# A recurrent block computed as three rounded products in place of one full one, with both halves of its input projection ahead of the gates

## The chip, the cores and the metric

The kernel runs on one core of one Trainium2 chip. The metric is the device time in microseconds (us), lower is better. One launch computes everything.

## The reference, cut to what matters

Two pairs of blocks follow each other over 512 tokens of width 1024, in float32. The first block is a recurrent mixer; a token's `h` is its normed input with a scale and a shift that depend on a condition vector `c` (the modulation).

```
mod = cond @ ada_w[i] + ada_b[i]             # six vectors of 1024: shift, scale, gate, twice
h = rmsnorm(x, norm_mix_g[i]) * (1.0 + sc1) + sh1
u = h @ w_in                                 # 1024 -> 2560
xb, gb = jnp.split(u, 2, axis=-1)
gate = jax.nn.gelu(gb)
xc = conv(xb, 4 taps) + conv_b
r = sigmoid(xc @ wr + br);  i = sigmoid(xc @ wi + bi)      # five blocks of 256 x 256
a = exp(-8 * r * softplus(-lam))
b = sqrt(1 - a*a) * (i * xc)
hs[t] = a[t] * hs[t-1] + b[t]
x = x + g1 * ((hs * gate) @ w_out)           # 1280 -> 1024
```

A feed-forward block, a sparse attention block and another feed-forward block follow; then an "even" block (768 tokens, latent and context: input projection of 21 tiles, a convolution of five taps, silu, and a norm of each head), its attention parts, an odd block and two more feed-forward blocks.

## The kernel before

Features lie on the 128 partitions and tokens along the row, so a tensor of 1280 features is ten tiles of 128 x 512. Each stage is a function that returns five programs, one for each engine's queue (`sp`, `pe`, `act`, `dve`, `pool`); a queue runs in the order in which it is written, and all order between engines is by semaphores (`st.at(event)`). So the order of the calls is the schedule. The weights stream through two slots of 2 MB (`panels`), 32 tiles of 128 x 128 each, in the order of `weight_plan`; a slot is loaded again when its last reader is done.

There are two kinds of matrix product. `linear` multiplies float32 by float32: one MATMUL in the code, two records in the profile. `linear3`, `turn3` and `opening3` multiply numbers split in a rounded high part and a rest (type fp32r): high by high, high by rest, rest by high, three MATMULs, one record each. For these the weights are made ready in groups of eight tiles: ACT rounds a group (`Halves.act`, one instruction of 128 x 1024) and POOL subtracts to get the rest in the weight slot itself (`HalvesInPlace.pool`, one instruction of 128 x 1024). Before the change every big projection but the recurrent block's `a_in` (20 output tiles by 8) and `a_out` (8 by 10) is of the second kind.

The recurrent block (`rglru`) before, on PE: eight products for the norm's sum; `a_in` tiles 0 to 3 in two halves of the inner index (L821), tiles 4 to 9 (L563); the gates, 20 outputs of two products each (L833); `a_in` tiles 10 to 19 (L563), the gelu branch; `a_out` (L563). DVE has the modulation (`Modulation.dve`, L396: two long multiply-and-sum instructions for each of 24 halves), the scaling of h, the taps of the convolution (L943, L946), and after the gates `gated_x` (L950), `m_product` (L955), the recurrence (L958 and the scan L960), and the end of gelu and its product with the scan (L963, L965). ACT has the gates' tanh (L884), two more functions of each (L889, L891), the roots (L894) and gelu's tanh (L900). POOL squares `a` (L982) and makes gelu's argument (L987, L989, L991). The scans, and gelu's work, run while PE is at tiles 10 to 19. 

In the even block a tile passes through ACT (copy, first tap), DVE (four taps, L2064), ACT (tanh), DVE (silu, L2070), and then the norm of its heads, `hn`: a square on ACT (L1414), a sum on PE (L1423), logarithm and exponential on ACT (L1432, L1435, with an exchange of the function table ahead of and behind them, L1995 and L2011), a product on DVE (L1442). `hn` for tile `i` stands on ACT in the round of tile `i + 2`, on PE ahead of the products of tile `i + 3` and on DVE in the round of tile `i + 3`. ACT copies tile `mt + 1` out of its bank only when it has squared tile `mt`.

Of the kernel before, what the change touches and what calls it, by code (L numbers as in the profile page):

```python
# [7 lines left out]
F32 = mybir.dt.float32  # L8
# [20 lines left out]
def weight_plan():  # L29
# [21 lines left out]
    stat("a_in", 10, 8)  # L51
# [4 lines left out]
    stat("a_in", 10, 8, 10)  # L56
    stat("a_out", 8, 10)
# [257 lines left out]
SPLIT = ("b_in", "b_out", "f1_0", "f2_0", "f1_1", "f2_1", "g_0", "u_0", "d_0", "g_1", "u_1", "d_1", "e_in", "e_out", "o_in", "nav", "gv", "o_out")  # L315
# [30 lines left out]
class Modulation:  # L346
# [19 lines left out]
    def landed(self, t):  # L366
        return (self.early[t][1], 16) if t < len(self.early) else (self.sems[t % 2], 16 * (self.base + t // 2 + 1))

    def sp(self, e, at):

        t = at["t"]
        if t < 2 * len(self.jobs):
            if t >= len(self.early) + 2:
                e.wait_ge(*self.st.at("half", t - 2))
            q = self.jobs[t // 2][0]
            e.load(self.slot(t), self.d_ada[q, :, (t % 2) * 2048:(t % 2 + 1) * 2048]).then_inc(self.landed(t)[0], 16)
            at["t"] += 1

    def dve(self, v, at, D):
# [4 lines left out]
        j, half = divmod(t, 2)  # L384
# [19 lines left out]
def program(nc, d_w, d_ada, d_const, d_rope, d_par, d_cond, d_rpb, d_x, d_ctx, d_out):  # L404
    with ExitStack() as es:
# [116 lines left out]
        def modulation(st, jobs, early=()):  # L522
            return Modulation(st, jobs, tiles, d_ada, ada_landed, early)
# [244 lines left out]
        def rglru(mod):  # L768
            st = stage("rglru")
            P, A, D, G = st.all  # L770
            H, SQ = tiles(8, S), tiles(2, S)
            XB = tiles(10, S + 3)
            later = pos[0]
            XCV, HS, M = tiles(10, S), tiles(10, S), tiles(10, S)
            AA = [x[:, 0:S] for x in XB]
            jobs = mod_jobs(0, [(conds[0], lambda: st.at("cond", 0))])
            fill = modulation(st, [jobs[q] for q in (0, 2, 1, 3)] + jobs[4:],
                              [(SB[:, later + 2048 * i:later + 2048 * (i + 1)], sem(f"ada_early{i}")) for i in range(6)])
            silu = alloc(1024)
            gs = small(8)  # L780
            c4, z, z2, s, m_, n4 = (small(10) for _ in range(6))
            hb = small(20)
            ring = (0, 1, 2, 3, 4, 5)
# [3 lines left out]
            def sp(e):  # L787
# [3 lines left out]
                for _ in range(4):  # L791
                    fill.sp(e, at)
                panels(e, "a_in", 0, 0, 1)
                for _ in range(4):
                    fill.sp(e, at)
                for mt in rows:
                    panels(e, "a_in", 7, mt)
                    fill.sp(e, at)
                for f in range(8):
                    e.load(XC[f], d_ctx[f, :, :]).then_inc(ctx_landed, 16)  # L800
                for f, g in gates:
                    panels(e, g, f // 2 * 2 + 1, f % 2)
                    if g == "gr":
                        fill.sp(e, at)
                for mt in rows:
                    panels(e, "a_in", 7, 10 + mt)
                for mt in range(8):
                    panels(e, "a_out", 9, mt)

            def pe(e):  # L810
# [4 lines left out]
                for half in range(2):  # L815
                    for mt in range(4):
                        for k in range(4 * half, 4 * half + 4):
                            t, landed = W.tile("a_in", k, mt)
                            e.wait_ge(*landed)
                            e.wait_ge(*st.at("h", k))  # L820
                            ins = e.mm(banks[ring[mt]], t, H[k], k == 0, k == 7)  # L821
                            if k == 7:
                                ins.then_inc(*P.up(("mm", mt), *W.done("a_in", k, mt)))
                g = linear(e, st, 4, ring, "a_in", rows[4:], 8, H, LAT, lambda k, lo: [])
# [11 lines left out]
                g = linear(e, st, g, ring, "a_in", range(10, 20), 8, H, LAT, lambda k, lo: [])  # L836
# [2833 lines left out]
```

## Time and profile before

| what | us |
|---|---|
| median of three runs (3492.33 to 3495.5) | 3494.76 |
| the profiled execution: its own time | 3495.64 |
| the profiled execution: span of the profile | 3493.8 |
| PE busy in it | 3252.5 (93%) |
| recurrent block, first instruction to its last product | 283.4 |
| even block's input stage, 1305.8 to 1527 | about 221 |

The own time is that of the whole execution, the span runs from its first to its last instruction. The granted clock of the profiled execution is 0.971 of full speed on average. Busy PE is not PE at its peak, so stretches are judged by start to start.

### The profile page before, as it was taken

What the parts mean: (1) busy time and instruction counts of PE and PEld (TensorE: products, weight loads), DVE (VectorE), ACT (ScalarE), POOL (GpSimd) and SP (SyncE); (2) the same over time, 40 slices, a digit from 0 to 9 for tenths busy, and PEclk for the clock granted to TensorE, in tenths of its full rate; (3) what the DMA queues carried; (4) which work ended last, traced back from release to release, by engine and by line L of the source; (5) the groups of instructions that cost most, each with busy time, mean ns of one, the idle gap of its engine ahead of it and who ended that gap; (6) DMA issues with size and microseconds to landing.
All of it is one profiled execution on the core that took longest, in us unless ns stands there. A gap on an engine that the chain in (4) does not pass through costs nothing.

```text
span 3493.8 us, 44613 instructions
## 1 busy us (share of the span) xinstructions
PE 3252.5 (93%) x18228; PEld 2549.8 (73%) x18228; DVE 1724.8 (49%) x3140; ACT 1278.9 (37%) x2273; POOL 1179.4 (34%) x963
## 2 busy tenths in 40 slices
PE   7999999887899998989899988999999998999998
PEld 3346888655678876755688876888887777868886
DVE  7744446588466677624566544122224318741223
ACT  2413233347432236625523234211213436743222
POOL 0233444542144442221265323222322342044443
PEclk9999999999999999999999999999999999999999
DMA  7513555310155542100122121111111111012221
GB/s 302 193 72 151 206 206 207 128 49 1 73 205 205 205 181 104 49 26 1 43 56 54 40 85 49 49 73 49 73 73 49 55 50 66 1 68 98 99 98 73
DMA packets 82412, 337.23 MB, mean 97 GB/s; under 512 B 46432, under 2 KB 50208, under 8 KB 57376
## 3 DMA queue, kind: packets, MB, share of 16 engines
q1 hardware_dynamic: 81344, 332.14, 25.5%
q8 instruction: 144, 2.36, 0.3%
q10 hardware_dynamic: 864, 2.24, 0.2%
q14 instruction: 60, 0.49, 0.0%
HBM read 326.64 MB, written 7.70 MB: 96 GB/s over the span
## 4 chain that ended last, share of the span: by engine, by line
PE 71%; DVE 15%; ACT 5%; POOL 4%; DMA 2%; issue 2%; SPq 1%; POOLq 0%; DVEq 0%; ACTq 0%
PE PSB L676 17%; PE PSB L680 17%; PE PSB L677 17%; PE PSB L1272 2%; PE PSB L1294 2%; PE PSB L563 2%; PE PSB L1281 2%; DVE SB L2064 2%; DVE SB L396 1%; DVE SB L1366 1%; DMA SB<-in_ada 1%; PE PSB L1833 1%; DVE SB L1382 1%; POOL SB L2924 1%; POOL SB L2922 1%
## 5 line engine op out<-in xcount | busy, mean ns | idle before, releaser
L680 PE MATMUL PSB<-R,WSR 128*128 128x512 f32 (+1 forms) x3084 | 1014.6, 366 | 0.0
L621 POOL TENSOR_TENSOR WSR<-SB,ahead 128x1024 fp32r<-128x1024 f32 x182 | 436.4, 2399 | 710.2 <-ACT ahead L598 674.7
L676 PE MATMUL PSB<-R,ahead 128*128 128x512 f32 (+1 forms) x1664 | 612.3, 368 | 2.5 <-POOL WSR L621 2.4
L677 PE MATMUL PSB<-R,ahead 128*128 128x512 f32 (+1 forms) x1664 | 592.7, 366 | 0.0
L680 PEld LDWEIGHTS PSB<-R,WSR 128*128 128x128 f32 x3084 | 533.6, 189 | 65.8
L676 PEld LDWEIGHTS PSB<-R,ahead 128*128 128x128 f32 x1664 | 312.8, 188 | 73.9 <-issue 3.5
L621 POOL TENSOR_TENSOR WSR<-SB,ffn_weights 128x1024 fp32r<-128x1024 f32 x96 | 230.2, 2398 | 388.8 <-ACT ffn_weights L598 388.8
L677 PEld LDWEIGHTS PSB<-R,ahead 128*128 128x128 f32 x1664 | 313.0, 188 | 52.7 <-issue 0.7
L676 PE MATMUL PSB<-R,ffn_weights 128*128 128x512 f32 x868 | 324.4, 374 | 7.0 <-POOL WSR L621 7.0
L677 PE MATMUL PSB<-R,ffn_weights 128*128 128x512 f32 x868 | 316.9, 373 | 0.0
L598 ACT ACTIVATE ahead<-SB 128x1024 fp32r<-128x1024 f32 x164 | 172.8, 1055 | 350.2 <-PE PSB L680 262.0
L396 DVE CUSTOM_DVE_ANT_0 SB<-SB,PSB 128x1024 f32<-128x1024 f32 x240 | 293.5, 1275 | 2.0 <-DMA SB<-in_ada 2.0
L3130 DVE SCALAR_TENSOR_TENSOR SB<-SB,PSB 128x512 f32<-128x512 f32 x66 | 39.4, 597 | 515.3 <-PE PSB L680 504.0
L676 PEld LDWEIGHTS PSB<-R,ffn_weights 128*128 128x128 f32 x868 | 163.3, 188 | 44.0 <-POOL WSR L621 8.5
L677 PEld LDWEIGHTS PSB<-R,ffn_weights 128*128 128x128 f32 x868 | 163.4, 188 | 28.9
L563 PE MATMUL PSB<-SB 128*128 128x512 f32 x416 | 179.2, 592 | 0.4 <-DVE SB L965 0.4
L598 ACT ACTIVATE ffn_weights<-SB 128x1024 fp32r<-128x1024 f32 x96 | 101.2, 1055 | 190.0 <-PE PSB L680 170.4
L563 PEld LDWEIGHTS PSB<-SB 128*128 128x128 f32 x416 | 78.8, 190 | 100.5 <-issue 98.8
L3097 ACT ACTIVATE R<-SB 128x512 fp32r<-128x512 f32 x66 | 37.0, 561 | 296.4 <-DVE SB L3132 296.4
L1281 PE MATMUL PSB<-SB 128*128 128x128 f32 x768 | 120.5, 284 | 24.7 <-DVE SB L1382 14.6
L3145 DVE TENSOR_TENSOR SB<-SB,PSB 128x512 f32<-128x512 f32 x120 | 68.9, 596 | 135.5 <-PE PSB L680 114.6
L1317 ACT ACTIVATE SB<-PSB 128x256 f32<-128x256 f32 (+3 forms) x272 | 116.4, 467 | 51.8 <-PE PSB L1281 51.1
(441 smaller groups left out, 5761.2 us busy)
## 6 DMA issues: line engine op xcount, KB each, us to landing
SB<-in_w SPq DMA_DIRECT2D x95, 2048.0 KB, 7.7
SB<-in_ada SPq DMA_DIRECT2D x96, 1024.0 KB, 4.9
SB<-gate_rows SPq DMA_DIRECT2D x12, 512.0 KB, 3.7
SB<-in_rpb SPq DMA_DIRECT2D x8, 448.0 KB, 4.2
spill<-SB SPq DMA_DIRECT2D x1, 3072.0 KB, 9.7
SB<-gate_rows SPq DMA_DIRECT2D x24, 128.0 KB, 3.7
SB<-spill SPq DMA_DIRECT2D x1, 3072.0 KB, 10.0
SB<-in_x SPq DMA_DIRECT2D x8, 256.0 KB, 6.4
```

Source lines behind the costliest of these rows:

```text
L396: v.ttr(out, w, cond, 1.0, bias[:, x:x + 1], ALU.mult, ALU.add, MOD[:, x * m + i:x * m + i + 1]).then_inc(*D.up(("half", t), ("mod", j), * ...
L563: ins = e.mm(banks[ring[(g + c) % len(ring)]][0:m, 0:n], t[:, 0:m], xs[k][:, lo:lo + n], k == 0, k == nkt - 1)
L598: e.act(hr, t, ACT.Copy).then_inc(*A.up(("hi", self.e0 + j)))
L621: e.tt(lr, t, hf, ALU.subtract).then_inc(*G.up(("lo", self.e0 + j)))
L676: e.mm(b[:, 0:n], wh, xh[:, lo:lo + n], x == 0, False)
L677: e.mm(b[:, 0:n], wh, xl[:, lo:lo + n], False, False)
L680: ins = e.mm(b[:, 0:n], wl, xh[:, lo:lo + n], False, last)
L1272: e.mm(ps[:, lo:lo + n], q, k, x == 0, x == len(steps) - 1).then_inc(*P.up(("score", s)))
L1281: e.tr(self.tbanks[u % 2][:, j:j + 128], self.SB_[t % 4][:, lo + j:lo + j + 128], ident).then_inc(*P.up(("transposed", u), ("p_read", t)))
L1294: e.mm(self.obanks[k % len(self.obanks)][par(hh), at:at + 128], self.V(2 * p + hh, b, j), self.PT[(2 * pair + hh) % 3][:, col(j)], j == 0, ...
L1317: e.act(self.PT[t % 3][:, lo:lo + n], self.tbanks[u % 2][:, 0:n], ACT.Copy).then_inc(*A.up(("tbank", u), ("p_T", t)))
L2064: v.stt(x, pd[:, off - 2 + j:off - 2 + j + n], w(j), x, ALU.mult, ALU.add).then_inc(*D.up(("conv", g)))
```

## The change

Five edits, four of them in the recurrent block.

1. `a_in` and `a_out` join the list `SPLIT` and are computed as three fp32r products. So h is made in two parts (ACT writes the high part, L918, DVE the rest), 20 + 10 groups of weights are rounded on ACT (L603) and have their rest made on POOL (L626), and y, the input of `a_out`, is also split: ACT rounds it (L898), POOL subtracts (L1110). Four buffers hold rounded groups.
2. Both halves of `a_in` stand ahead of the gates on PE. gelu's work goes with the second half: argument and end on DVE (L1043, L1049), square and tanh on ACT, none on POOL. The first tap of the convolution goes from DVE to ACT.
3. After the gates stands the recurrence with the product by gelu in the same round (L1058, L1060, L1062), and right behind it `a_out`. Its first two output tiles are taken together over the inner index (`turn3`), in the order in which the ten y come.
4. The modulation's halves come in another order (the first pair of h needs two halves, not four), into other buffers: 8 are summed ahead of h, 8 within gelu, 3 within the gates, 5 within `a_out`. Context tiles are loaded a stage later. softplus stands first on DVE.
5. In the even block `hn` stands one tile later on PE, ACT and DVE.

```diff
-    stat("a_in", 10, 8)
+    stat("a_in", 20, 8)
...
-    stat("a_in", 10, 8, 10)
-    stat("a_out", 8, 10)
+    plan.extend(("a_out", k, m) for k in range(10) for m in range(2))
+    stat("a_out", 6, 10, 2)
...
-                g = linear(e, st, 4, ring, "a_in", rows[4:], 8, H, LAT, lambda k, lo: [])
+                g = linear3(e, st, 4, ring, front, "a_in", rows[4:], range(8), H, LAT, lambda x, lo: [])
+                g = linear3(e, st, g, ring, back, "a_in", range(10, 20), range(8), H, LAT, lambda x, lo: [])
...
-                g = linear(e, st, g, ring, "a_in", range(10, 20), 8, H, LAT, lambda k, lo: [])
-                linear(e, st, g, ring, "a_out", range(8), 10, HS, LAT, lambda k, lo: [st.at("gated", k)])
+                ready = lambda x, lo: [st.at("y", x)]
+                g = turn3(e, st, g, ring, last, "a_out", (0, 1), range(10), YH, LAT, ready)
+                linear3(e, st, g, ring, last, "a_out", range(2, 8), range(10), YH, LAT, ready)
...
+                for mt in range(11):
+                    if mt < 10:
+                        ps = banks[ring[(10 + mt) % 6]]
+                        e.wait_ge(*st.at("mm", 10 + mt))
+                        e.act(U[mt], ps, ACT.Copy).then_inc(*A.up(("u", mt)))
+                        if mt >= 2:
+                            e.wait_ge(*st.at("gelu", mt - 2))
+                        e.act(SQ[mt % 2], ps, ACT.Square, scale=0.044715 ** 0.5).then_inc(*A.up(("bank", 10 + mt), ("u_square", mt)))
+                        back.act(e, A, mt + 2)
...
+                    if 3 <= f < 6:
+                        e.wait_ge(*st.at("group_used", 13 + f))
+                        last.act(e, A, f - 3)
+                    if f == 7:
+                        roots(range(5))
+                roots(range(5, 10))
...
+                for mt in range(11):
+                    if mt < 10:
+                        t = SQ[mt % 2]
+                        v.wait_ge(*st.at("u_square", mt))
+                        v.stt(t, t, 1.0, U[mt], ALU.add, ALU.mult).then_inc(*D.up(("gelu_arg", mt)))
+                    if mt < 8:
+                        fill.dve(v, at, D)
+                    if mt:
+                        t = SQ[(mt - 1) % 2]
+                        v.wait_ge(*st.at("gelu_tanh", mt - 1))
+                        v.stt(U[mt - 1], t, 1.0, U[mt - 1], ALU.add, ALU.mult).then_inc(*D.up(("gelu", mt - 1)))
...
+                def scan(f):
                     v.wait_ge(*st.at("m_sqrt", f))
                     v.stt(M[f], M[f], 0.5, HS[f], ALU.mult, ALU.mult).then_inc(*D.up())
                     v.wait_ge(*D.now())
                     v.scan(HS[f], AA[f], M[f], 0.0, ALU.mult, ALU.add).then_inc(*D.up(("scan", f)))
...
+                    v.stt(HS[f], U[f], 0.5, HS[f], ALU.mult, ALU.mult).then_inc(*D.up(("gated", f)))
...
+                for f in rows:
+                    if f in (2, 5, 8):
+                        fill.dve(v, at, D)
+                    v.wait_ge(*st.at("gate", 2 * f + 1))
+                    v.wait_ge(*st.at("mm", 20 + 4 * (f // 2) + 3))
+                    v.stt(HS[f], M[f], 1.0, XCV[f], ALU.add, ALU.mult).then_inc(*D.up(("gated_x", f)))
+                    if f >= 2:
+                        m_product(f - 2)
+                    if f == 9:
+                        scan(0)
...
+                for k in rows:
+                    e.wait_ge(*st.at("y_hi", k))
+                    e.tt(YH[k][2], HS[k], high_of_y[k][0], ALU.subtract).then_inc(*G.up(("y", k)))
...
-                    if 3 <= mt < 11:
-                        hn.pe(e, P, mt - 3)
+                    if 4 <= mt < 12:
+                        hn.pe(e, P, mt - 4)
...
-                        if 2 <= mt < 10:
+                        if 3 <= mt < 11:
                             e.tables(LOG_EXP)
-                            hn.act(e, A, mt - 2)
+                            hn.act(e, A, mt - 3)
```

What stands on POOL in the recurrent block before, from its start (L977 clears the edge of the convolution's tiles, L982 squares `a`, L987 to L991 are gelu's argument; the last three rows repeat ten times):

```order
L977 MEMSET SB 128x3 x10
L982 ISA
L982 TENSOR_TENSOR SB<-SB 128x512 x10
L987 TENSOR_TENSOR SB<-SB 128x512
L989 TENSOR_SCALAR SB<-SB 128x512
L991 TENSOR_TENSOR SB<-SB 128x512
```

And of the change, from the gelu branch's last groups on (L626 makes the rest of a weight group, L1105 squares `a`, L1110 makes the rest of y):

```order
L626 TENSOR_TENSOR WSR<-SB,rglru_weights 128x1024 x2
L1105 TENSOR_TENSOR SB<-SB 128x512 x4
L626 TENSOR_TENSOR WSR<-SB,XCR 128x1024
L1105 TENSOR_TENSOR SB<-SB 128x512
L626 TENSOR_TENSOR WSR<-SB,XCR 128x1024
L1105 TENSOR_TENSOR SB<-SB 128x512
L626 TENSOR_TENSOR WSR<-SB,rglru_weights 128x1024
L1105 TENSOR_TENSOR SB<-SB 128x512 x4
L1110 TENSOR_TENSOR rglru_rests<-SB,rglru_rounded 128x512 x10
```

POOL's queue holds 30 of the long instructions now, 20 within `a_in`, three between the gates' squares, seven behind the rests of y.

DVE within the gelu branch of the change, one round (L1043 is gelu's argument, the four L401 one half of the modulation, L1049 gelu's end for the tile before):

```order
L1043 SCALAR_TENSOR_TENSOR SB<-SB 128x512
L401 ISA SB<-SB 128x1024
L401 ISA SB 128x1
L401 ISA SB<-SB 128x1024
L401 ISA SB 128x1
L1049 SCALAR_TENSOR_TENSOR SB<-SB 128x512
```

And DVE of the change from its last `gated_x` (L1069) on, where before ten L955 stood and then rounds of L958 and L960 alone:

```order
L1069 SCALAR_TENSOR_TENSOR SB<-SB 128x512
L1054 SCALAR_TENSOR_TENSOR SB<-SB 128x512
L1058 SCALAR_TENSOR_TENSOR SB<-SB 128x512
L1060 SCALAR_TENSOR_TENSOR SB<-SB 128x512
L1062 SCALAR_TENSOR_TENSOR SB<-SB 128x512
L1054 SCALAR_TENSOR_TENSOR SB<-SB 128x512 x2
L1058 SCALAR_TENSOR_TENSOR SB<-SB 128x512
L1060 SCALAR_TENSOR_TENSOR SB<-SB 128x512
L1062 SCALAR_TENSOR_TENSOR SB<-SB 128x512
```

The first recurrence moved into the gates' last round, and the product by gelu (L1062) into each round; `a_out` no longer has tiles 10 to 19 between itself and the gates.

## Rows read from the trace of the kernel before

**Rows 1.** The page: the chain that ended last, by engine.

```profile
PE 71%; DVE 15%; ACT 5%; POOL 4%; DMA 2%; issue 2%; SPq 1%; POOLq 0%; DVEq 0%; ACTq 0%
```

**Rows 2.** Stretches: us, busy of PE, PEld, DVE, ACT, POOL, granted clock, DMA, GB/s.

```profile
29.50:59.40 29.90, 29.90 (x65) 13.21 (x66) 19.86 (x52) 10.83 (x15) 0.00 (x0) 0.92 0.64 267
...
103.60:145.20 41.60, 34.31 (x75) 14.05 (x74) 29.23 (x46) 20.44 (x30) 3.63 (x2) 0.96 0.58 223
145.20:214.70 69.50, 69.50 (x164) 30.75 (x163) 54.44 (x48) 24.89 (x39) 44.71 (x35) 1.00 0.24 91
```

**Rows 3.** The chain in `a_out`; then weight loads at two three-product steps.

```profile
222.09 61.33 PE PSB L563 x142
...
340.31 0.19 PEld L676 LDWEIGHTS PSB<-R,ffn_weights 128*128 128x128 f32 x1
...
340.99 0.19 PEld L676 LDWEIGHTS PSB<-R,ffn_weights 128*128 128x128 f32 x1
```

**Rows 4.** Groups, 0 to 480 us: count, busy us, mean ns, idle before.

```profile
L598 ACT ACTIVATE ahead<-SB 128x1024 fp32r<-128x1024 f32 x24 | 25.4, 1057 | 48.0 <-PE PSB L680 46.2 <-DMA SB<-in_w 1.7
...
L621 POOL TENSOR_TENSOR WSR<-SB,ahead 128x1024 fp32r<-128x1024 f32 x24 | 57.5, 2394 | 123.3 <-ACT ahead L598 123.3
...
L396 DVE CUSTOM_DVE_ANT_0 SB<-SB 128x1024 f32<-128x1024 f32 x48 | 59.7, 1282 | 12.6 <-DMA SB<-in_ada 12.6
...
L1171 DVE SCALAR_TENSOR_TENSOR SB<-PSB,SB 128x512 f32<-128x512 f32 x16 | 12.0, 751 | 42.4 <-PE PSB L680 42.4
...
L846 ACT ACT_TABLE_LOAD x2 | 2.6, 1283 | 2.2 <-issue 2.1
```

**Rows 5.** POOL beside DVE at two places: start, us, what.

```profile
120.57 1.28 DVE L396 CUSTOM_DVE_ANT_0 SB<-SB 128x1024 f32<-128x1024 f32 x1
...
120.65 2.10 POOL L982 TENSOR_TENSOR SB<-SB 128x512 f32<-128x512 f32 x1 [2.33 <-ACT SB L891]
...
1392.80 2.38 POOL L621 TENSOR_TENSOR WSR<-SB,XCR 128x1024 fp32r<-128x1024 f32 x1 [9.36 <-ACT XCR L598]
...
1393.37 2.37 DVE SB L2064
```

**Rows 6.** ACT in order of time, the end of the first norm.

```profile
23.30 0.58 ACT L743 ACTIVATE PSB<-PSB 128x512 f32<-128x512 f32 x1
```

**Rows 7.** DVE in order of time, two rounds of the gates.

```profile
140.61 0.69 DVE L950 SCALAR_TENSOR_TENSOR SB<-SB 128x512 f32<-128x512 f32 x1 [2.88 <-ACT SB L884]
144.18 0.69 DVE L950 SCALAR_TENSOR_TENSOR SB<-SB 128x512 f32<-128x512 f32 x1 [2.88 <-ACT SB L884]
```

**Rows 8.** DVE in order of time, one round of the recurrence.

```profile
165.34 0.68 DVE L958 SCALAR_TENSOR_TENSOR SB<-SB 128x512 f32<-128x512 f32 x1
166.05 1.23 DVE L960 TENSOR_TENSOR_SCAN SB<-SB 128x512 f32<-128x512 f32 x1
```

**Rows 9.** PE in the feed-forward block's first products, after an idle spell.

```profile
290.94 0.77 PE L702 MATMUL PSB<-R,ahead 128*128 128x512 f32 x1 [4.10 <-DVE R L1024]
...
297.04 0.39 PE L705 MATMUL PSB<-R,WSR 128*128 128x512 f32 x1
297.27 0.39 PE L702 MATMUL PSB<-R,ahead 128*128 128x512 f32 x1
```

**Rows 10.** The chain in the even block's input stage: start, us, what.

```profile
1347.93 2.39 DVE SB L2064
...
1358.76 2.34 DVE SB L2064
...
1369.87 2.40 DVE SB L2064
...
1430.97 1.72 PE PSB L1423 x4
...
1435.50 0.35 PE PSB L680 x2
1436.54 0.35 PE PSB L680 x2
```

More of the change, by code:

```diff
@@ L383, in dve @@
         at["t"] += 1
-        j, half = divmod(t, 2)
+        j, half = divmod(self.order[t], 2)
         _, conds, bias, MOD = self.jobs[j]
@@ L520, in program, with modulation @@
         assert LATER >= 3072
-        def modulation(st, jobs, early=()):
-            return Modulation(st, jobs, tiles, d_ada, ada_landed, early)
+        def modulation(st, jobs, early=(), first=(), after=()):
+            return Modulation(st, jobs, tiles, d_ada, ada_landed, early, first, after)
         def mod_jobs(i, cs, first=0, end=12):
@@ L770, in rglru @@
             P, A, D, G = st.all
-            H, SQ = tiles(8, S), tiles(2, S)
+            rows_at = pos[0]
+            H, SQ = pairs(8, S), tiles(2, S)
+            early = [pos[0]]
             XB = tiles(10, S + 3)
+            pos[0] = -(-pos[0] // 64) * 64
             later = pos[0]
-            XCV, HS, M = tiles(10, S), tiles(10, S), tiles(10, S)
+            early += [later + 2048 * i for i in range(5)]
+            XCV, M = tiles(10, S), tiles(10, S)
+            HS = XCV
+            low_of_y, high_of_y = ([rounded_tiles(f"rglru_{x}{k}", 1, S, at + k * S)[0] for k in range(10)]
+                                   for x, at in (("rests", later), ("rounded", later + 10 * S)))
@@ L775, in rglru @@
+            YH = [(None, high_of_y[k][1], low_of_y[k][1]) for k in range(10)]
             AA = [x[:, 0:S] for x in XB]
             jobs = mod_jobs(0, [(conds[0], lambda: st.at("cond", 0))])
-            fill = modulation(st, [jobs[q] for q in (0, 2, 1, 3)] + jobs[4:],
-                              [(SB[:, later + 2048 * i:later + 2048 * (i + 1)], sem(f"ada_early{i}")) for i in range(6)])
-            silu = alloc(1024)
+            gelu_at = pos[0]
+            U = tiles(10, S)
+            silu = SB[:, gelu_at + 8 * S:gelu_at + 10 * S]
@@ new lines, in rglru @@
+            room.update({t: ("mm", 19) if t < 20 else ("half", t - 4) for t in range(16, 24)})
+            fill = modulation(st, [jobs[q] for q in (0, 2, 1, 3)] + jobs[4:], early, (0, 2, 1, 3, 4, 6, 5, 7), room)
+            assert pos[0] % 64 == 0
+            WS = rounded_tiles("rglru_weights", 2, GROUP * 128)
+            XS = [(XCR[:, i * 1024:(i + 1) * 1024].bitcast(F32), XCR[:, i * 1024:(i + 1) * 1024]) for i in range(2)]
+            of_in = [t for t in W.plan if t and t[0] == "a_in"]
+            front = HalvesInPlace(st, of_in[0:80], WS + XS)
@@ L780, in rglru @@
+            back = HalvesInPlace(st, of_in[80:160], WS + XS, 10)
+            last = HalvesInPlace(st, [t for t in W.plan if t and t[0] == "a_out"],
+                                 XS + WS, 20)
             gs = small(8)
@@ L879, in act, with roots @@
+                e.wait_ge(*st.at("half", 15))
+                e.wait_ge(*st.at("half_bias"))
+                e.wait_ge(*st.at("lam"))
+                g = 20
+                def roots(fs):
+                    for f in fs:
+                        e.wait_ge(*st.at("m_product", f))
+                        e.act(M[f], M[f], ACT.Sqrt).then_inc(*A.up(("m_sqrt", f)))
                 for f in rows:
@@ L955, in dve @@
                     v.stt(M[f], SQ[f % 2], 1.0, M[f], ALU.add, ALU.mult).then_inc(*D.up(("m_product", f)))
-                for f in rows:
+                def scan(f):
                     v.wait_ge(*st.at("m_sqrt", f))
```

216 lines of the change are left out of this document (132 added, 84 removed).

## The prediction

> **What bounds the kernel now.** I read the page first: the chain that ended last is 71% PE and 15% DVE [rows 1], so a PE microsecond mostly counts, but not everywhere. Then the recurrent block by stretch [rows 2]: PE has `a_in` tiles 0 to 3 from 29.5 to 59.4, tiles 4 to 9 to 103.6, the gates to 145.2 (PE busy 34.3 of 41.6), and from 145.2 it is never idle until the scans have ended; the last product of `a_out` ends at 283.4. In 145.2 to 214.7 DVE is busy for 54.4 us and POOL for 44.7 [rows 2]: recurrence and gelu lie under PE's work there. That is the cover which the change takes away. Last, I looked at what POOL and DVE do to each other, and at the even block's chain.
>
> **Products.** A float32 product takes 61.33 / 71 = 0.864 us (two records each), three rounded ones 0.68 [rows 3]. 240 products change: PE's own work falls by 240 x 0.18 = 44 us. If PE were the bound all along, this would be the gain.
>
> **What it costs POOL.** 30 groups of weights need 1.06 us each on ACT and 2.39 each on POOL [rows 4], the rests of y some 1.2 each (half of 2.39, being half as long). On POOL this is 84 us, against gelu's work that leaves it. How this meets DVE, rows show. L396, which reads two SBUF tensors, ran from 120.57 to 121.8; POOL's L982 beside it took 2.10 us, about 1.0 of it after L396's end. And L2064 was ready at 1393.37 while POOL's L621 ran to 1395.18; it ended at 1395.74 [rows 5], 0.6 later, where such an instruction alone takes 0.68 [rows 8]. So a POOL instruction and a DVE one that reads two SBUF operands take turns, and the one that waits gets in at the next gap. DVE's instructions with an operand in PSUM are free of this (L1171 mean 0.75, beside L621 [rows 4]). I walk the queues of the recurrent block with these prices and this turn-taking, 0.06 us for a hand-over between engines.
>
> The Trainium skill (SBUF — State Buffer, section "SBUF: two separate sides") states the same as a rule, an exclusive lock for the whole instruction. It speaks against this change; by it the walk gives what stands below, and without it the first rival. The trace agrees, as told.
>
> **Opening: +5 us.** For each of four pairs of h: DVE has two halves of modulation, each two L396 (four take 4.9 [rows 4]), two scalings and two rests of 0.67, and 0.7 in which ACT makes the high part: 8.9 us. The first pair's halves are summed by the time the norm is there, 23.9 [rows 6], as they also are before (softplus, some 5 us of small instructions, goes ahead of them into DVE's wait for its first operands); it is done at 27.9; three more take 26.7, and of POOL's first four groups two to three stand in DVE's way, 5 us: h 7 is there at 59. PE needs 5.4 us more: tiles 0 to 3 end at 64.3, before at 59.4.
>
> **Tiles 4 to 9: 32.7 us.** A tile is 8 x 0.68 = 5.44. ACT (2.3) and POOL with the taps on DVE (2.4 + 2.3) fit. To 97.0; before to 103.6.
>
> **Tiles 10 to 19: 66 us instead of 54.** In eight of the ten rounds this closes a loop: ACT square 0.6, DVE argument 0.69, one L396 1.21, POOL's rest of the next weights 2.38, the other L396 1.21, gelu's end 0.69 and two hand-overs, 6.9 us, since ACT squares tile mt only when gelu mt - 2 is done, and stands ahead of the next weights' rounding. 2 x 5.44 + 8 x 6.9 = 66: `a_in` ends at 163. Before, this branch ended at 214.7 but behind the gates.
>
> **Gates: 53.5 us to the last `gated_x`.** They run at ACT's pace now, 3.57 us a round [rows 7], against PE's 3.46. In the change the first `gated_x` also waits for PE's fourth output, 6.9 us; nine rounds give 32.1. Three groups of weights, each 1.06 on ACT and 2.39 on POOL in front of a `gated_x`, add 2.3 each, 6.9; three halves of modulation 1.9 net; five roots within round 7, with two table exchanges of 1.28 [rows 4], 5.2. Sum 53.0 to 53.5: last `gated_x` at 216.5.
>
> **Recurrence: uncovered, 43 us.** A round is 0.71 + 1.25 + 0.68 = 2.64 [rows 8], plus the rest of the y before it on POOL, 1.2: 3.83. From the last `gated_x` to the end of the first round 5.1, the last two `m_product` 1.4, nine rounds 34.5, then ACT's rounding, POOL's rest and two products 3.9: 261.4. Under this PE has only `turn3`'s twenty products, 13.6 us. Behind it the queue holds 60 products of `a_out`, 40.8: 302.2. PE is less than half busy in these rounds; after such a spell it ran 14 products in 6.1 us, at the lower of its two levels, where then 0.22 each are normal [rows 9], so 3 us more: 305.2.
>
> Against 283.4, the recurrent block is 21.8 us longer: 44 saved in products, and PE's idle time from its first product on up from 12 (7.3 of it in the gates) to 78. Moving ctx loads costs nothing: SP has slack there. ACT's part (first taps, y) hides under PE; uncovered it would be 0.6 a tile, 6 us. Whatever follows starts later by the same amount.
>
> **The even block: +2.4.** The loop ACT to DVE bounds until its round 8: 10.83 us without `hn`, 11.11 in the first round with it, then 11.75 [rows 5, 10]. The wait of PE at 1430.97 for the logarithm of round 8 is the last; then PE runs alone, 8.4 us a tile (1.04 a step of eight) [rows 10]. With `hn` a round later this wait is for round 9: one more round, less 0.9 as rounds 2 and 3 get the lighter price, 10.8; and one tile less is behind it, 8.4. Bounds: 0 if PE's last wait turns out to be elsewhere, +3.4 if rounds 2 and 3 keep their price.
>
> **Sum.** 21.8 + 2.4 = 24.2 on the profiled execution's own 3495.6 makes 3519.8; the median of the runs lies 0.9 under it: 3519.
>
> **Rivals.**
> - *Faster: the turns cost nothing in the end.* If POOL's instructions fall into DVE's pauses, the same walk without them gives: tiles 0 to 3 at 57.4, `a_in` done at 144.5, the first two tiles of `a_out` at 223.5, the end at 264.3 + 3. That is 16 under before; with the even block 3481. Taking turns is worth 38 us in the walk, so it decides the sign where less than 14 of them arise. For it: POOL's and DVE's queues have pauses of 1 to 3 us in a round of the gates [rows 7]. Against: in the loop of tiles 10 to 19 and in the recurrence neither has a pause, and these alone are 12 + 11 of the 38. 14%.
> - *About the same.* The eight rounds run at 5.44 to 6.2 since the rest of the weights slips into the time of ACT's square (up to -9), and the groups within the gates are made while DVE waits for PE (-6), and h comes 5 sooner. Sum about +4: 3499. 14%.
> - *Slower still.* PE falls to its lower level within the gates too, where a round of PE takes 6.9 instead of 3.46 and outlasts ACT's. In the gates of before the clock was 0.96 with PE busy for 82% [rows 2]; here it has 34.6 of 53. If half the rounds fall, +15: 3534. 8%.
> - *The change doesn't do what it says:* excluded for the products, each is written out; for the even block's step see its bounds.
>
> **How the numbers follow.** The forecast has 62%, 3506 to 3530: its own errors are the rounds of tiles 10 to 19 (5.44 or 6.9, 12 us), y's rest (1.2, at most the 1.0 to 2.1 that POOL took for 512 columns in these rows: up to +4) and the first panel's landing (+4). What a measurement of this kernel can tell from no change is about 0.2%, 7 us: under 3488 is faster, over 3502 slower. Range 3490 to 3536. Faster 0.15 (the first rival and a tail), the same 0.13 (most of the second), slower 0.72.
>
> **What would show it in the profile.** Right: PE idle for some 45 us between the gates' start and the third tile of `a_out`; rounds of L1058, L1060, L1062 of 3.8 us with an L1110 in each; tiles 16 to 19 nearly 7 us apart, with L401 stretched beside L626; the end of `a_out` near 305; in the even block the last wait at L1423's line about 11 us later than now. Wrong: L626 at 2.4 without a wait beside L401 and L401 at 1.2 throughout, or `a_in` done by 150, or y coming every 2.7 us. The prediction falls above all if the turn-taking is dodged, or if work of the recurrence begins while the gates still run, beyond its first round.

## The result, and the profile of the changed kernel

The changed kernel takes 3505.78 us (median of six runs, 3503.79 to 3509.49), the kernel before 3495.13 beside it: a ratio of 1.0029, 95% interval 1.0019 to 1.0039. Run again beside the experiments it took 3503.57 against 3496.47, a ratio of 1.0025 (1.0016 to 1.0033). So it is slower, by 7 to 11 us as the two pairs of medians have it (9 to 10 by the ratios), and not by the 24 of the forecast. Its profiled execution has an own time of 3506.28 and a span of 3504.4, 10.6 over before.

The page of the changed kernel, the chain that ended last, by engine, beside [rows 1]:

```profile
PE 73%; DVE 15%; ACT 6%; POOL 2%; issue 2%; DMA 1%; SPq 1%; ACTq 0%; POOLq 0%; DVEq 0%
```

Stretches of the recurrent block after the change, columns as in [rows 2]: `a_in` tiles 0 to 3, 4 to 9, 10 to 19; the gates, as a whole and in two parts; the recurrence; `a_out` from its third tile on.

```profile
29.50:65.00 35.50, 26.13 (x93) 19.23 (x94) 30.86 (x41) 9.51 (x14) 12.24 (x15) 0.80 0.40 167
65.00:98.50 33.50, 33.46 (x147) 27.11 (x145) 32.20 (x26) 20.06 (x26) 17.23 (x7) 1.00 0.46 178
98.50:159.70 61.20, 56.84 (x242) 44.73 (x242) 54.09 (x56) 24.64 (x37) 27.92 (x9) 1.00 0.47 178
159.70:209.00 49.30, 34.88 (x81) 14.72 (x79) 27.47 (x32) 36.72 (x52) 20.08 (x12) 0.92 0.53 213
...
159.70:200.80 41.10, 34.88 (x81) 14.72 (x79) 25.24 (x28) 29.82 (x43) 19.04 (x11) 1.00 0.64 255
200.80:209.00 8.20, 0.00 (x0) 0.00 (x0) 2.23 (x5) 6.90 (x11) 1.04 (x1) 0.50 0.00 0
...
209.00:248.00 39.00, 23.91 (x55) 15.00 (x55) 38.31 (x37) 13.59 (x20) 22.19 (x11) 0.58 0.00 1
248.00:291.00 43.00, 42.36 (x186) 34.73 (x186) 32.10 (x31) 11.53 (x15) 23.00 (x8) 1.00 0.39 147
```

The number behind POOL's busy time is the granted clock. In 159.7 to 248 PE is busy for 58.8 of 88.3 us, so idle for 29.5, where some 45 were foretold. As long as it has products of the gates the clock is at the upper of its two levels (1.00); it falls at 200.8, when PE has been without work for about 5 us, and of the recurrence's 23.9 us of busy time most is at the lower one. The last product of `a_out` ends at 290.4, before at 283.4 (read here and below as the start of the addition that waits for it): the recurrent block is 7.0 us longer. This is carried on: the first DVE instruction of the feed-forward block (L1285) stands at 311.5, before at 304.9; the even block's input stage ends at 1534.0, before at 1527.9, 6.1 later. The last 4.4 of the 10.6 arise behind it, in stages that the edits don't touch ("The last 4 us", below).

One round of tiles 10 to 19 on DVE (start, us, engine, line, what), and POOL beside it:

```profile
123.88 0.69 DVE L1043 SCALAR_TENSOR_TENSOR SB<-SB 128x512 f32<-128x512 f32 x1 [0.67 <-ACT SB L946]
124.48 1.28 DVE L401 CUSTOM_DVE_ANT_0 SB<-SB 128x1024 f32<-128x1024 f32 x1
125.69 3.39 DVE L401 CUSTOM_DVE_ANT_0 SB<-SB 128x1024 f32<-128x1024 f32 x1
129.01 0.68 DVE L1049 SCALAR_TENSOR_TENSOR SB<-SB 128x512 f32<-128x512 f32 x1
130.36 0.69 DVE L1043 SCALAR_TENSOR_TENSOR SB<-SB 128x512 f32<-128x512 f32 x1 [0.67 <-ACT SB L946]
...
124.87 3.12 POOL L626 TENSOR_TENSOR WSR<-SB,rglru_weights 128x1024 fp32r<-128x1024 f32 x1 [3.35 <-ACT rglru_weights L603]
```

POOL's L626 waits some 0.7 us for the first L401's end, and the second L401 then lasts 3.39 us instead of 1.28: it ends 1.1 us after POOL. The round is 6.48 us, PE's own work in it 5.44 (a tile of eight steps of three products).

In the gates ACT makes the pace; DVE and POOL there:

```profile
177.70 0.69 DVE L1069 SCALAR_TENSOR_TENSOR SB<-SB 128x512 f32<-128x512 f32 x1 [2.28 <-ACT SB L966]
182.21 1.84 DVE L1069 SCALAR_TENSOR_TENSOR SB<-SB 128x512 f32<-128x512 f32 x1 [3.22 <-ACT SB L966]
187.88 0.69 DVE L1069 SCALAR_TENSOR_TENSOR SB<-SB 128x512 f32<-128x512 f32 x1 [0.81 <-ACT SB L966]
188.49 2.85 DVE L1054 SCALAR_TENSOR_TENSOR SB<-SB 128x512 f32<-128x512 f32 x1
192.39 0.69 DVE L1069 SCALAR_TENSOR_TENSOR SB<-SB 128x512 f32<-128x512 f32 x1 [1.05 <-ACT SB L966]
...
181.16 2.35 POOL L626 TENSOR_TENSOR WSR<-SB,XCR 128x1024 fp32r<-128x1024 f32 x1
187.92 2.87 POOL L626 TENSOR_TENSOR WSR<-SB,XCR 128x1024 fp32r<-128x1024 f32 x1
```

Of the three groups of weights in the gates only the first stands in the way of a `gated_x` (L1069), for 1.15 us. The other two, at 187.92 and 192.48, each hold an `m_product` (L1054), 2.85 us instead of 0.68. That costs the next `gated_x` nothing: after the one at 188.49 DVE still waits 1.05 us for ACT. And the recurrence:

```profile
225.33 1.22 DVE L1060 TENSOR_TENSOR_SCAN SB<-SB 128x512 f32<-128x512 f32 x1
226.59 1.58 DVE L1062 SCALAR_TENSOR_TENSOR SB<-SB 128x512 f32<-128x512 f32 x1
228.09 0.68 DVE L1058 SCALAR_TENSOR_TENSOR SB<-SB 128x512 f32<-128x512 f32 x1
...
225.44 2.18 POOL L1110 TENSOR_TENSOR rglru_rests<-SB,rglru_rounded 128x512 fp32r<-128x512 f32 x1 [1.29 <-ACT rglru_rounded L898]
```

POOL's rest of y waits for the scan; then the product by gelu (1.58, alone 0.68) waits for POOL: 0.9 us in each round of 3.47.

### The profile page after: what moved, and what is told of

It is laid out like the page before. It is cut to its first block, busy times and chain, and to the rows that moved or that the text cites. A ratio compares the mean times of both kernels' runs of the same rounds, so it can differ in the third digit from the quotient of the medians.

```text
span 3504.4 us, 45184 instructions
## 1 busy us (share of the span) xinstructions
PE 3231.8 (92%) x18468; PEld 2607.8 (74%) x18468; DVE 1779.5 (51%) x3150; ACT 1326.5 (38%) x2334; POOL 1247.5 (36%) x973
## 3 DMA queue, kind: packets, MB, share of 16 engines
q8 instruction: 146, 2.39, 0.3%
## 4 chain that ended last, share of the span: by engine, by line
PE 73%; DVE 15%; ACT 6%; POOL 2%; issue 2%; DMA 1%; SPq 1%; ACTq 0%; POOLq 0%; DVEq 0%
PE PSB L681 18%; PE PSB L685 18%; PE PSB L682 18%; PE PSB L1396 2%; PE PSB L1418 2%; PE PSB L1405 2%; DVE SB L2188 2%; DVE SB L401 1%; DVE SB L1490 1%; DVE SB L1506 1%; DVE PSB L1139 1%; DVE R L1145 1%; PE PSB L1957 1%; DVE SB L1801 1%; DVE SB L1799 1%
## 5 line engine op out<-in xcount | busy, mean ns | idle before, releaser
L685 PE MATMUL PSB<-R,WSR 128*128 128x512 f32 (+1 forms) x3212 | 1064.4, 367 | 0.0
L626 POOL TENSOR_TENSOR WSR<-SB,ahead 128x1024 fp32r<-128x1024 f32 x182 | 436.1, 2397 | 661.0 <-ACT ahead L603 625.6
L685 PEld LDWEIGHTS PSB<-R,WSR 128*128 128x128 f32 x3212 | 557.4, 189 | 70.7
L626 POOL TENSOR_TENSOR WSR<-SB,ffn_weights 128x1024 fp32r<-128x1024 f32 x96 | 230.1, 2397 | 385.4 <-ACT ffn_weights L603 385.4
L603 ACT ACTIVATE ahead<-SB 128x1024 fp32r<-128x1024 f32 x164 | 172.8, 1055 | 354.3 <-PE PSB L685 257.0
L401 DVE CUSTOM_DVE_ANT_0 SB<-SB,PSB 128x1024 f32<-128x1024 f32 x240 | 293.5, 1274 | 2.6 <-DMA SB<-in_ada 2.6
L603 ACT ACTIVATE ffn_weights<-SB 128x1024 fp32r<-128x1024 f32 x96 | 101.2, 1055 | 188.9 <-PE PSB L685 164.7
L1405 PEld LDWEIGHTS PSB<-SB 128*128 128x128 f32 x768 | 89.7, 144 | 45.3 <-DVE SB L1506 27.5
L1285 DVE TENSOR_TENSOR PSB<-PSB,SB 128x512 f32<-128x512 f32 x64 | 44.6, 696 | 149.6 <-ACT SB L1241 149.6
```

Of the source, the lines that this page charges most:

```text
L401: v.ttr(out, w, cond, 1.0, bias[:, x:x + 1], ALU.mult, ALU.add, MOD[:, x * m + i:x * m + i + 1]).then_inc(*D.up(("half", t), ("mod", j), * ...
L603: e.act(hr, t, ACT.Copy).then_inc(*A.up(("hi", self.e0 + j)))
L626: e.tt(lr, t, hf, ALU.subtract).then_inc(*G.up(("lo", self.e0 + j)))
L685: ins = e.mm(b[:, 0:n], wl, xh[:, lo:lo + n], False, last)
L1405: e.tr(self.tbanks[u % 2][:, j:j + 128], self.SB_[t % 4][:, lo + j:lo + j + 128], ident).then_inc(*P.up(("transposed", u), ("p_read", t)))
```

## The experiments

Each kernel was timed in four to twelve runs; a ratio is always to runs of the kernel before on the same chip, whose median was 3496.5 to 3497.7.

### Take the turns away: condition row in PSUM

```diff
-            fill = modulation(st, [jobs[q] for q in (0, 2, 1, 3)] + jobs[4:], early,
+            row = PSB[:, 6 * 512:8 * 512]
+            in_psum = mod_jobs(0, [(row, lambda: st.at("row"))])
+            fill = modulation(st, [jobs[q] for q in (0, 2, 1, 3)] + in_psum[4:], early,
...
+                    if mt == 7:
+                        e.wait_ge(*st.at("h", 7))
+                        e.act(row, conds[0], ACT.Copy).then_inc(*A.up(("row",)))
```

> The change, but the modulation's long instructions from the ninth half on read the condition row from two free PSUM banks (one copy on ACT in tile 7 of a_in, 1 us). Theory A, turn-taking of two-SBUF-operand DVE instructions with POOL: L401 is free of POOL in tiles 10 to 19, POOL's rest falls from 3.1 to 2.4 us, the eight rounds fall from 6.48 to PE's 5.44 and a_in ends 8 us sooner; some 8 us off the whole (about 3498). Rival B, the loop through ACT sets these rounds whatever POOL does: L401 at 1.3 but rounds of 6.3 to 6.5, whole within 2 us of the change.

Measured: 3497.3, ratio 0.9995 (0.9985 to 1.0005). DVE in tiles 10 to 19 of this kernel, POOL beside it, and three `gated_x` (L1074 here):

```profile
125.49 0.69 DVE L1048 SCALAR_TENSOR_TENSOR SB<-SB 128x512 f32<-128x512 f32 x1 [1.49 <-ACT SB L951]
126.10 1.27 DVE L401 CUSTOM_DVE_ANT_0 SB<-SB,PSB 128x1024 f32<-128x1024 f32 x1
127.30 1.27 DVE L401 CUSTOM_DVE_ANT_0 SB<-SB,PSB 128x1024 f32<-128x1024 f32 x1
128.50 0.94 DVE L1054 SCALAR_TENSOR_TENSOR SB<-SB 128x512 f32<-128x512 f32 x1
130.93 0.69 DVE L1048 SCALAR_TENSOR_TENSOR SB<-SB 128x512 f32<-128x512 f32 x1 [1.49 <-ACT SB L951]
...
126.48 2.41 POOL L626 TENSOR_TENSOR WSR<-SB,XCR 128x1024 fp32r<-128x1024 f32 x1 [3.03 <-ACT XCR L603]
...
173.75 1.84 DVE L1074 SCALAR_TENSOR_TENSOR SB<-SB 128x512 f32<-128x512 f32 x1 [3.22 <-ACT SB L971]
179.41 1.84 DVE L1074 SCALAR_TENSOR_TENSOR SB<-SB 128x512 f32<-128x512 f32 x1 [0.82 <-ACT SB L971]
185.08 1.84 DVE L1074 SCALAR_TENSOR_TENSOR SB<-SB 128x512 f32<-128x512 f32 x1 [3.22 <-ACT SB L971]
```

L401 and L626 now run at the same time at 1.27 and 2.41, and the round is 5.44. Gelu's last argument starts at 152.7 instead of 160.9: 8.2 us where theory A said 8, and rival B is out. But at the last `gated_x` only 6.2 of it are left (202.4 against 208.6). In the change one `gated_x` waits for a group's rest; here three do. In the change an L401 held POOL's square of `a` up (2.13 us instead of 1.04 at 185.83), and so the group behind it; now the group starts sooner, where `gated_x` is due. `a_out` is done at 283.9, 6.5 us under the change. At the feed-forward block's first DVE instruction (304.9) the kernel is level with before.

### The rest of y without POOL

```diff
-                    v.stt(HS[f], U[f], 0.5, HS[f], ALU.mult, ALU.mult).then_inc(*D.up(("gated", f)))
+                    v.stt(YP[f % 4], U[f], 0.5, HS[f], ALU.mult, ALU.mult).then_inc(*D.up(("gated", f)))
+
+                def y_rest(f):
+                    v.wait_ge(*st.at("y_hi", f))
+                    v.tt(YH[f][2], YP[f % 4], high_of_y[f][0], ALU.subtract).then_inc(*D.up(("y", f)))
```

> The change, but the product by gelu writes y to a PSUM bank, and DVE makes its rest from there (0.66 us, ahead of the scan) instead of POOL. Theory A: POOL's 0.86 stood in DVE's way in full, so a round goes from 3.47 to 0.68 + 0.66 + 1.24 + 0.68 = 3.26: 2 us sooner at the last y, 2 off the whole. Rival B, POOL's rest ran beside DVE and something else (semaphores, ACT) fills the round: the round gets longer by 0.66 less what it hides, 3.5 to 4.1, and the whole is 0 to 6 us slower than the change.

Measured: 3498.72, ratio 1.0006 (0.9997 to 1.0016). A round of this kernel's recurrence on DVE:

```profile
224.43 0.68 DVE L1059 SCALAR_TENSOR_TENSOR SB<-SB 128x512 f32<-128x512 f32 x1
225.18 0.69 DVE L1070 TENSOR_TENSOR rglru_rests<-PSB,rglru_rounded 128x512 fp32r<-128x512 f32 x1
225.79 1.21 DVE L1064 TENSOR_TENSOR_SCAN SB<-SB 128x512 f32<-128x512 f32 x1
227.03 0.70 DVE L1066 SCALAR_TENSOR_TENSOR PSB<-SB 128x512 f32<-128x512 f32 x1
```

It is 3.22 us long, 0.25 less than in the change: DVE now makes the rest itself, in 0.69 with the hand-over hidden, and is rid of the 0.9 for which it waited for POOL. So POOL's rest stood in its way in full, as theory A has it. The last rest starts 1.8 us sooner and the last product of `a_out` ends 2.1 sooner. The whole moved by more than that, from 1.0025 to 1.0006, which these edits don't explain: in this kernel's profile the even block's input stage ends at 1538.3, 4.3 us later than in the change, and what follows takes 11.8 less, all in unchanged code.

### Undo the order: gates ahead of tiles 10 to 19

```diff
-    stat("a_in", 20, 8)
+    stat("a_in", 10, 8)
...
+    stat("a_in", 10, 8, 10)
...
-                g = linear3(e, st, g, ring, back, "a_in", range(10, 20), range(8), H, LAT, lambda x, lo: [])
                 for f, name in gates:
...
+                g = linear3(e, st, g, ring, back, "a_in", range(10, 20), range(8), H, LAT, lambda x, lo: [])
```

The diff is cut to the order. The kernel also has both relocations of the two sections above, gelu's squares in PSUM besides, and other places for the modulation's halves (six in the gates, ten in `a_out`). On DVE the scan of tile `mt`, gelu's argument of `mt`, gelu's end and y of `mt - 1` and the rest of `mt - 2` now make one round.

> Rounded products kept, the order undone: gates between tiles 0 to 9 and 10 to 19 of a_in, so that gelu and the recurrence lie under tiles 10 to 19; gelu's squares and y in PSUM, condition row in PSUM, y's rests on DVE, six halves of modulation in the gates, ten in a_out. Theory C, lost cover is what eats the 44 us: tiles 4 to 9 end at 98, gates to 141, tiles 10 to 19 take 54 to 60, a_out 54: it ends at 250 to 256 instead of 290, the whole about 3470, some 25 under the kernel before. Rival D, DVE and POOL bound the block in either order: tiles 10 to 19 and the recurrence take 75 or more behind the gates, a_out ends at 270 or later, the whole 3485 or more.

Measured: 3465.19, ratio 0.9909 (0.9896 to 0.9923). The last product of `a_out` ends at 256.1, 34.3 sooner than in the change, and theory C had said 250 to 256. What was left in the way, DVE and POOL in a round of this kernel (L1074 is y):

```profile
176.03 0.68 DVE L1072 SCALAR_TENSOR_TENSOR SB<-PSB,SB 128x512 f32<-128x512 f32 x1
176.74 2.27 DVE L1074 SCALAR_TENSOR_TENSOR PSB<-SB 128x512 f32<-128x512 f32 x1
...
176.06 2.41 POOL L627 TENSOR_TENSOR WSR<-SB,rglru_weights 128x1024 fp32r<-128x1024 f32 x1 [3.57 <-ACT rglru_weights L604]
```

L1072, with an operand in PSUM, runs beside POOL at its 0.68; L1074, with both of its inputs in SBUF, waits until POOL's end, although it writes to PSUM. So the next kernel orders DVE's round by that: y of `mt - 2`, b and scan of `mt` (two operands in SBUF) first, the rest of that y, gelu's end of `mt - 1` and argument of `mt` (one in PSUM) behind them. On ACT the rounding of the next group goes ahead of the square:

```diff
-                        if mt >= 2:
-                            e.wait_ge(*st.at("y", mt - 2))
-                        e.act(TB[mt % 2], ps, ACT.Square, scale=0.044715 ** 0.5).then_inc(*A.up(("bank", 30 + mt), ("u_square", mt)))
                         e.wait_ge(*st.at("group_used", 10 + mt))
                         if mt < 6:
                             back.act(e, A, mt + 4)
                         else:
                             last.act(e, A, mt - 6)
+                        if mt >= 2:
+                            e.wait_ge(*st.at("y", mt - 2))
+                        e.act(TB[mt % 2], ps, ACT.Square, scale=0.044715 ** 0.5).then_inc(*A.up(("bank", 30 + mt), ("u_square", mt)))
```

> The gates-first kernel with DVE's round in another order: its three instructions on two SBUF operands (y, b, scan) first, its three with a PSUM operand (y's rest, gelu's end and argument) last and next to each other, ACT's rounding of the weights so that POOL's 2.4 us begin as the scan ends; four halves of modulation in the gates in place of six, weight groups there a round sooner. In the gates-first kernel y's product took 2.27 us in place of 0.68, waiting for POOL, and a round 5.97. Theory A: y's product at 0.7 to 0.9, the round at PE's 5.44, a_out ends 5 to 9 us sooner (near 249), the whole about 3458. Rival: POOL and DVE share something whatever the operands, rounds stay at 5.9 and the whole within 3 us of the gates-first kernel, but for the 3 us that the gates may save.

DVE and POOL in a round of this kernel (L1059 is y, L1062 b, L1067 the rest of y, L1071 and L1074 gelu):

```profile
175.01 1.41 DVE L1059 SCALAR_TENSOR_TENSOR PSB<-SB 128x512 f32<-128x512 f32 x1
176.33 0.68 DVE L1062 SCALAR_TENSOR_TENSOR SB<-SB 128x512 f32<-128x512 f32 x1
177.04 1.22 DVE L1064 TENSOR_TENSOR_SCAN SB<-SB 128x512 f32<-128x512 f32 x1
178.18 0.67 DVE L1067 TENSOR_TENSOR rglru_rests<-PSB,rglru_rounded 128x512 fp32r<-128x512 f32 x1
178.77 0.68 DVE L1071 SCALAR_TENSOR_TENSOR SB<-PSB,SB 128x512 f32<-128x512 f32 x1
179.50 0.70 DVE L1074 SCALAR_TENSOR_TENSOR PSB<-PSB,SB 128x512 f32<-128x512 f32 x1
...
178.56 2.40 POOL L627 TENSOR_TENSOR WSR<-SB,rglru_weights 128x1024 fp32r<-128x1024 f32 x1 [2.70 <-ACT rglru_weights L604]
```

Measured: a round of 5.1 (under PE's 5.44, since DVE started behind PE and was catching up), `a_out` done at 249.2 (6.9 sooner, and 34.2 under before), y's product at 1.41 since three instructions don't quite cover POOL's 2.40. The whole is 3462.11, ratio 0.9901 (0.9887 to 0.9914), only 3 under the one before it, with overlapping intervals: the place moved as theory A said, and 4 of its 7 us can't be found again in the whole.

The change's own order with both relocations into PSUM (the condition row, and y with its rest on DVE) tells whether these or the order made it quick.

> The change in its own order with both relocations to PSUM at once: condition row for L401, and y with its rest on DVE. If the two gains are separate they add: a_out's last tile at 290.4 less 6.5 less 2.1, near 282, and the whole some 3494. If the order itself is what costs, it stays 28 to 34 us above the gates-first kernels (3465 and 3462), which have the same two relocations. If instead the relocations made those quick, it comes within 10 of them.

Measured: 3496.15, ratio 0.9997 (0.9987 to 1.0007), `a_out` done at 282.8. The two gains add, to within 1 us (290.4 less 6.5 and 2.1 is 281.8), and the gates-first kernels end 27 and 34 us sooner still. PE around tiles 10 to 19 of this kernel (some 2 us more at each end), columns as in [rows 2]:

```profile
96.00:154.00 58.00, 58.00 (x253) 47.23 (x252) 41.02 (x57) 25.15 (x40) 23.78 (x10) 1.00 0.53 204
```

It never waits there, so gelu's squares in PSUM, which this kernel lacks, could have won nothing. From 96 to 283 PE is idle for 36.2 us, in the gates-first kernel from 98 to 256 for 10.0: that is 26 of the 27 us. The difference is the cover that PE's own work gives the recurrence in the other order. The further 7 are the aligned round and four instead of six halves in the gates, which no run separates.

### Move POOL's groups out of the gates

```diff
-                    if 3 <= f < 6:
-                        e.wait_ge(*st.at("group_used", 13 + f))
-                        last.act(e, A, f - 3)
...
                 roots(range(5, 10))
+                e.wait_ge(*st.at("group_used", 18))
+                for j in range(3):
+                    last.act(e, A, j)
```

> The change with the first three weight groups of a_out moved out of the gates: ACT rounds them behind the roots, POOL makes their rests ahead of y's rests. In the gates they cost some 4 us in the trace of the change, not my 6.9, since ACT and DVE pause there. Theory A (a POOL instruction costs DVE its whole length only where DVE has no pause): the last gated_x is 3 to 4 us sooner, but the 7.2 us of POOL now stand in the recurrence, where DVE has none, so the last y's rest is 2 to 4 us later than in the change and the whole 2 to 4 slower. Rival B (the groups cost the same anywhere): the last y within 1 us of the change.

Measured: 3506.76, ratio 1.0028 (1.0017 to 1.0039). The last `gated_x` starts at 205.0 instead of 208.6. Then in the recurrence:

```profile
212.64 2.69 DVE L1062 SCALAR_TENSOR_TENSOR SB<-SB 128x512 f32<-128x512 f32 x1
215.26 2.83 DVE L1058 SCALAR_TENSOR_TENSOR SB<-SB 128x512 f32<-128x512 f32 x1
218.12 3.24 DVE L1060 TENSOR_TENSOR_SCAN SB<-SB 128x512 f32<-128x512 f32 x1
```

Three instructions in a row wait for one group each, about 2 us each time. The last rest of y starts at 249.2 instead of 246.3, `a_out` ends at 293.3 instead of 290.4. So the same three groups, with their rounding on ACT, cost 3.6 us where DVE waits for ACT anyway, and 6.5 (3.6 won, 2.9 lost) where it has no pause. Theory A held in both places. The whole is 3.2 us above the change's second median (3503.57, the same chip), as theory A had it, though the intervals overlap.

### The even block's head norm

The fifth edit undone in the change:

> The change with its fifth edit undone: in the even block the head norm stands where it stood before (PE and DVE mt - 3, ACT mt - 2). By my prediction's term the whole is 2.4 us quicker than the change. By the trace of the change it is 0, within 0.5 in the trace: the last wait of PE comes 1.3 us sooner in the change, and one more sum of squares of 1.3 us stands behind it. Where the head norm should matter in some other way, over 3 us either way.

The fifth edit alone in the kernel before:

> The kernel before with the change's fifth edit alone, the head norm one tile later. By my prediction's term: 2.4 us slower. By the trace of the change: the end of the even block's input stage moves by no more than 0.3 us (1.3 won in the rounds, 1.3 for one more sum of squares behind PE's last wait), and the whole within 3 us of before.

And undone in the aligned kernel:

> The gates-first kernel with DVE's order aligned, its head norm put back where before has it. If the head norm's step matters by itself, as the medians of the change (3503.6) and of the change without it (3499.1) might say, this is some 4 us quicker than the aligned one's 3462.1, and the gain again lies in the odd block. If that difference came from where the clock falls there, this one moves by up to 5 either way, with the even block's input stage unchanged within 0.5.

| kernel | whole | ratio (95%) | first taps to the stage's end |
|---|---|---|---|
| before | 3495.13 | | 190.7 |
| the change | 3505.78 | 1.0029 (1.0019 to 1.0039) | 190.7 |
| the change, norm back | 3499.1 | 1.0009 (1.0000 to 1.0018) | 190.4 |
| before, norm later | 3494.57 | 0.9995 (0.9986 to 1.0004) | 191.1 |
| aligned, norm later | 3462.11 | 0.9901 (0.9887 to 0.9914) | 190.7 |
| aligned, norm back | 3459.68 | 0.9893 (0.9879 to 0.9908) | 190.4 |

The last column runs from the first start of the taps' line to the addition that closes the input stage, 1337.2 to 1527.9 in before. In its place the step costs 0.3 to 0.5 us, not 2.4. Two sums of squares on PE in the changed kernel's chain (L1547) show why. PE starts the first when ACT has done its part, and it stands nowhere waiting behind the second:

```profile
1435.88 1.72 PE PSB L1547 x4
...
1446.02 1.29 PE PSB L1547 x4
```

The last long wait, before 1435.88, is for the same round of ACT as in before (1430.97 there), not for the next. Seven rounds take 78.3 us (1343.38 to 1421.72) and not 79.6 (1337.21 to 1416.83), which brings 1.3, and one more sum of squares (1.29) now stands behind that wait and takes it back. In the wholes the norm's old place looks better twice and worse once, by 2 to 7 us with intervals of 3 us to each side; that is not settled, and if it is real, it isn't in the even block's input stage.

### The last 4 us

> The change itself, run again beside the others. Its trace up to the end of the even block's input stage should come out as in the first, 6.1 us behind before (1534.0). Of its first profile's 10.6 us, 4.4 arose after that point, in code that both kernels share. If these 4.4 are where the granted clock happened to fall, they go or change here, and the median comes to 6 to 10 over before on the same chip; if they belong to the change, they are there again, at the same place.

> The kernel before with nothing but a delay: eight more float32 products into an unused bank at the end of the recurrent block (8 x 0.864 = 6.9 us; their result is not used). It stands in for the 7.0 us by which the change's recurrent block ended later. Theory F, the later stages only move along: the whole is 6.9 us slower than before (ratio 1.0020), and each mark behind it 6.9 later. Rival G, the odd block's input stage, where the granted clock falls for spells, takes another time when it starts elsewhere: that mark is 6.9 later up to 1700 us, and the rest differs by several us more, as the change's 4.4 did.

```diff
+                for _ in range(8):
+                    e.mm(banks[6], ones, HS[9], True, True)
                 square_sums_pe(e, P, st, H[0], H[2])
```

The change again: 3503.57, span 3504.5, the input stage's end at 1535.2, and the same late stretch as the first time. Before with a delay alone: 3501.95, ratio 1.0016 (1.0007 to 1.0025), so 5.6 us for the 6.9 put in, within the interval of theory F. But its profiled execution has a span of 3508.2, 14.4 over before's: 6.1 at the feed-forward block's first DVE instruction, 3.5 more by the even stage's end, 7.3 more by the end of the odd block's input stage, and 2.5 less in what follows. In this one execution, the longest of its twelve, rival G is nearer, though 3.5 of the extra us arise before the place that it named. In the odd block the clock falls for spells. A window 270 us behind the even stage's end, of before:

```profile
1797.90:1817.90 20.00, 17.86 (x268) 16.06 (x266) 13.16 (x22) 6.89 (x17) 11.83 (x33) 1.00 0.24 52
```

of the change:

```profile
1804.00:1824.00 20.00, 17.75 (x206) 16.20 (x207) 11.74 (x19) 5.64 (x15) 11.47 (x34) 0.87 0.25 55
```

and of before with a delay:

```profile
1807.50:1827.50 20.00, 17.88 (x200) 16.44 (x199) 12.36 (x19) 5.25 (x14) 11.16 (x33) 0.86 0.25 56
```

The number behind POOL's busy time is 1.00, 0.87 and 0.86; 120 us further on it is 1.00, 0.83 and 0.68.

From the even stage's end to the end of the span, the profiles of all these kernels take 1958.6 us (y in PSUM) to 1970.7 (before with a delay), though the code is the same; nearly all of the spread arises by the end of the odd block's input stage. The stretch ahead of it isn't fixed either: from the feed-forward block's first DVE instruction to the even block's first tap, unchanged code took between 1031.9 and 1038.7 us. So 4.4 us of one profile behind a changed stage is no effect of the change that could be shown. Whether a kernel's spells follow from when the block starts, or are drawn anew each run, these runs don't settle: the change had them in both of its profiles, before with a delay in its only one, which is 8 us over its median.

## Why the prediction was wrong in size

The sign and the mechanism held: the change ends later, since the recurrence lost its cover and POOL's instructions take turns with DVE's. The forecast of +24 was more than twice too large. In the stages that the edits touch it was off by still more: there it had 24.2, and 6.1 to 7.0 came. That the whole rose by 10.6 in the profiled execution is owed to 4.4 us that arose later and that the forecast had no term for. By its own steps, in the changed kernel's trace:

| step | predicted | measured |
|---|---|---|
| tiles 0 to 3 end | 64.3 | 65.4 |
| tiles 4 to 9 | 32.7 | 33.2 |
| tiles 10 to 19 | 66 | 61.1 |
| gates to the last `gated_x` | 53.5 | 48.8 |
| from there to PE's first product of the third tile of `a_out` | 44.9 | 40.7 |
| the rest of `a_out` | 43.8 | 41.1 |
| end of `a_out` | 305.2 | 290.4 |
| even block's step | +2.4 | +0.3 to +0.5 |

The step that failed is the pricing of the turns: the terms for the gates, for tiles 10 to 19 and for the recurrence charged instructions of POOL and ACT in full where part of them cost DVE nothing, and came out 4.7, 4.9 and 4.2 us too long. Two small terms, for the clock and for the even block, were for things that didn't happen.

**The gates' term** is the one where this is plainest: "three groups of weights, each 1.06 on ACT and 2.39 on POOL in front of a `gated_x`, add 2.3 each, 6.9; three halves of modulation 1.9 net". The intervals between the `gated_x` show 4.3 for all six. They cost ACT's 0.94 three times, POOL's overhang of 1.15 once and 0.28 for one half of the modulation; the rest lay where DVE would have waited for ACT. The second rival had said that this would happen, though with DVE waiting for PE and not for ACT. **The loop of tiles 10 to 19** was right in kind (6.48 a round, L401 stretched beside L626, 8.2 us gone when the turns are taken away), and 4.9 us too long in all. A round was charged 6.9, with both L401 and POOL's whole 2.38 one behind the other; POOL's instruction put only 2.1 between the two. And seven rounds ran in the loop, not eight: they took 45.4 us, the other three 15.7. **The recurrence** was charged 1.2 for each rest of y; it cost 0.9. **The clock's 3 us** didn't come: it was at the lower level from 200.8 to 241.8, as foreseen, but back at the upper one when the last y came. In the windows 218 to 228, 238 to 248 and 248 to 258 it is 0.50, 0.81 and 1.00. **The even block's term** put PE's last wait a round too late.

The third rival is out: the clock was at its upper level for as long as PE had products of the gates, and the 0.92 of that stretch comes from its end, where PE had none. One sum of the prediction doesn't come out: the items named for a pair of h make 8.3 us, not 8.9. All errors but two small ones (the first two rows) point the same way.

The Trainium skill (SBUF — State Buffer, section "SBUF: two separate sides") tells of an exclusive lock between a DVE instruction with two SBUF inputs and a GpSimd instruction that reads SBUF, held for the whole instruction. The rows agree: L1062 takes 1.58 us instead of 0.68 and ends 0.55 after POOL's L1110, and with one input in PSUM L1072 takes its 0.68 beside L627.

## What to carry to other kernels

A POOL instruction beside DVE costs what of it meets DVE work on two SBUF operands that has no pause around it: look for the pause first, then charge it. Move one input to PSUM (an output there did not help), or put the instructions that have one there next to each other, and begin POOL's work with them. Before work that was hidden is uncovered in exchange for cheaper products, count how long it is by itself: against the kernel before, the rounded products with the relocations into PSUM save 32 us with the gates first (38 after the round was aligned and the norm put back) and 1 in the change's order, which is no difference that the runs can tell.

## What was not expected

Taking one collision away made another: with L401 free of POOL, two more `gated_x` waited 1.15 us each. And the stages behind the even block's input, the same code in all kernels, differ by up to 12 us between profiles, mostly where the granted clock falls in the odd block, which is more than most edits here were worth.
